# Value products of a head pair made together, in alternating column halves, with four probability slots

## What is computed

```
lb = einsum('bthd,bshd->bhts', qb, k_b)
lb = lb + swapaxes(fq, 1, 2)[..., None] - cum_f_keys[:, :, None, :]
lb = where(causal[None, None], lb, -inf)
pb = softmax(lb, axis=-1)
ob = einsum('bhts,bshd->bthd', pb, v_b)
```

## Time and profile before

| | |
|---|---|
| median of 3 runs | 2182.43 us (2182.37 to 2182.81) |
| profiled execution | 2186.65 us |
| its span, first to last instruction | 2185.0 us |
| PE busy | 2060.1 us, 94% of the span |
| DVE busy | 1236.7 us, 57% |
| ACT busy | 910.8 us, 42% |
| POOL busy | 289.2 us, 13% |
| DMA | mean 89 GB/s |

### The profile page before, as it was taken

The page is one execution under the profiler, slowest core; times in us unless marked ns, Lnnn a source line. Parts: engine busy times, 40 slices in busy tenths (PEclk is TensorE's granted clock), DMA queues, the critical chain, the costliest instruction groups (busy, mean ns, idle before and its releaser), DMA issues. The chain is left out here.

```text
span 2185.0 us, 26996 instructions
## 1 busy us (share of the span) xinstructions
PE 2060.1 (94%) x9546; PEld 1634.7 (75%) x9546; DVE 1236.7 (57%) x1910; ACT 910.8 (42%) x1403; POOL 289.2 (13%) x380
## 2 busy tenths in 40 slices
PE   8999998999999999999999988898887998999997
PEld 6666666888888677688888857787765677888886
DVE  3666556888677565756664353766556544333333
ACT  4333735444322443544442254565446624222222
POOL 0032501011000010000000012666410001000000
PEclk9999999999999999999999999999998999999999
DMA  5511023666454322233233212011110022233321
GB/s 171 147 47 39 1 68 102 193 194 193 134 173 136 106 87 78 67 96 96 96 107 106 86 38 78 30 30 39 59 39 1 1 87 77 96 96 96 116 94 51
DMA packets 52779, 193.93 MB, mean 89 GB/s; under 512 B 5808, under 2 KB 8528, under 8 KB 52312
## 3 DMA queue, kind: packets, MB, share of 16 engines
q1 hardware_dynamic: 44824, 165.18, 23.9%
q0 software_dynamic: 7344, 27.27, 4.0%
q10 hardware_dynamic: 528, 0.40, 0.1%
HBM read 189.15 MB, written 3.68 MB: 88 GB/s over the span
## 5 line engine op out<-in xcount | busy, mean ns | idle before, releaser
L196 PE MATMUL psum<-xH,w_hi 128*128 128x512 f32 x1800 | 729.1, 405 | 42.8 <-DVE xL L1377 22.1
L196 PE MATMUL psum<-xL,w_hi 128*128 128x512 f32 x1800 | 712.1, 396 | 0.0
L196 PE MATMUL psum<-xH,w_lo 128*128 128x512 f32 x1800 | 711.7, 395 | 0.0
L166 DVE TENSOR_TENSOR w_lo<-w_raw,w_hi 128x1024 fp32r<-128x1024 f32 (+1 forms) x273 | 357.0, 1308 | 365.4 <-ACT w_hi L160 365.0
L160 ACT ACTIVATE w_hi<-w_raw 128x1024 fp32r<-128x1024 f32 (+1 forms) x273 | 303.3, 1111 | 420.1 <-PE psum L196 410.8
L196 PEld LDWEIGHTS psum<-xH,w_hi 128*128 128x128 f32 x1800 | 344.4, 191 | 142.0 <-DVE xL L1377 37.7
L196 PEld LDWEIGHTS psum<-xH,w_lo 128*128 128x128 f32 x1800 | 344.4, 191 | 74.1
L196 PEld LDWEIGHTS psum<-xL,w_hi 128*128 128x128 f32 x1800 | 344.8, 192 | 71.4 <-issue 3.1
L196 PE MATMUL psum<-hidH,w_hi 128*128 128x512 f32 x528 | 206.2, 391 | 0.0
L196 PE MATMUL psum<-hidH,w_lo 128*128 128x512 f32 x528 | 205.4, 389 | 0.0
L196 PE MATMUL psum<-hidL,w_hi 128*128 128x512 f32 x528 | 205.4, 389 | 0.0
(11 more groups left out here) (321 smaller groups left out, 2488.4 us busy)
## 6 DMA issues: line engine op xcount, KB each, us to landing
w_raw<-in_up SPq DMA_DIRECT2D x132, 512.0 KB, 3.5
w_raw<-in_down SPq DMA_DIRECT2D x48, 704.0 KB, 4.1
mod_raw<-in_mod POOLq DMA_DIRECT2D x48, 512.0 KB, 3.9
w_raw<-in_sb_in SPq DMA_DIRECT2D x26, 512.0 KB, 3.5
w_raw<-in_ev_in SPq DMA_DIRECT2D x23, 512.0 KB, 4.0
w_raw<-in_od_in SPq DMA_DIRECT2D x20, 512.0 KB, 3.5
w_raw<-in_ev_out SPq DMA_DIRECT2D x8, 512.0 KB, 3.6
w_raw<-in_od_out SPq DMA_DIRECT2D x8, 512.0 KB, 3.5
```

Of the source, the lines that this page charges most:

```text
L166: nc.vector.tensor_tensor(w_lo[:, s % SPLIT, 0:w.cols], raw[:, s, 0:w.cols], w_hi[:, s % SPLIT, 0:w.cols].bitcast(F32), ALU.subtract).then ...
L196: mm = nc.tensor.matmul(acc, a[:, slot % SPLIT, cut], b[:, k0 + k, :], start=start and n == 0, stop=stop and n == 2)
```

## The change

The value products of the two heads of a pair are made in one call, at the step of the second head (steps 6, 8, ... 36), with the matmuls of the two heads taking turns over the key blocks. `pv_b` counts pairs instead of units. The transposed probabilities get four slots instead of two: the two of `pTb`, and two in columns 1024 to 1279 of the four rows of `w_raw`. ACT's copy of unit u waits from unit 4 on, for the pair of unit u - 4.

```diff
+        pT_b = (pTb[:, 0, :, :], pTb[:, 1, :, :], raw[:, :, KD * P:(KD + 1) * P], raw[:, :, (KD + 1) * P:(KD + 2) * P])
+        assert NB == RAW and (KD + 2) * P <= CHUNK
...
                 def prob_out(u):
                     kind, i, h = units[u]
                     if kind == "b":
-                        dst = pTb[:, u % 2, 0:i + 1, :]
-                        if u >= 2:
-                            act.wait_ge(a["pv_b"], u - 1)
+                        dst = pT_b[u % 4][:, 0:i + 1, :]
+                        if u >= 4:
+                            act.wait_ge(a["pv_b"], u // 2 - 1)
...
                         m = (s - 13) // 8
-                        act.wait_ge(a["pv_b"], 8 * (m + 1))
+                        act.wait_ge(a["pv_b"], 4 * (m + 1))
...
-                def values_b(u):
-                    _, i, h = units[u]
-                    m = u // 8
-                    pe.wait_ge(a["prob_out"], u + 1)
-                    if u % 8 == 0 and m >= 2:
+                def values_b(n):
+                    _, i, h0 = units[2 * n]
+                    m = n // 4
+                    pe.wait_ge(a["prob_out"], 2 * n + 2)
+                    if n % 4 == 0 and m >= 2:
                         pe.wait_ge(a["o_b_hi"], m - 1)
                     for j in range(i + 1):
-                        mm = nc.tensor.matmul(bank[6 + m % 2][rows(h), blk(i)], v_tm[:, j, h * HD:(h + 1) * HD],
-                                              pTb[:, u % 2, j, :], start=j == 0, stop=j == i)
+                        for e in range(2):
+                            mm = nc.tensor.matmul(bank[6 + m % 2][rows(h0 + e), blk(i)], v_tm[:, j, (h0 + e) * HD:(h0 + e + 1) * HD],
+                                                  pT_b[2 * (n % 2) + e][:, j, :], start=j == 0, stop=j == i)
                     mm.then_inc(a["pv_b"], 1)
...
-                    if PV <= s < UNITS + PV:
-                        values_b(s - PV)
+                    if PV <= s < UNITS + PV and (s - PV) % 2:
+                        values_b((s - PV) // 2)
```

## The result

The changed kernel takes 2171.18 us in the median (five runs, 2169.34 to 2172.14), against 2182.43 of the kernel before in five runs beside it (2180.35 to 2183.41): a ratio of 0.9948, with a 95% interval of 0.9933 to 0.9962. That is 11.3 us less, between 8.3 and 14.6. The forecast was 2170.8.

A forecast was written before the change was run, and what follows sets the result against it. PE alone was taken to bound the kernel from 116 to 218 us. Gains of 9.6 us there and 2.0 us behind sum to 11.6, taken off the median 2182.43: 2170.8 us, range 2167 to 2175.

The forecast's parts named there:

- The time of a pair's call: Value products, line 858: calls of 4, 8, 12, 16 records take 0.36, 0.58, 0.80, 1.03 us.
- The rival at 137 ns a record: Value products: weight loads run in series at 137 ns, so no change, 2182.5 us; chance 0.02.
- The sum of the projection: Pairs 0 to 11, steps 5 to 27: three rounds of 3.27 us saved, less 0.2, gives 9.6 us.
- The shape changes around a call: Array shape switches before and after each value product call: 0.13 us of the 0.49 for 2 records.
- The second head: Other column half in a pair's call: nearly free, 0.02 us a call, 0.2 us for twelve.
- Pair 12: Step 29: gains nothing; up to 0.36 us goes, but filler matmuls wait for ACT to empty bank 1 at 218.15.
- The tail: Pairs 13 to 15 (steps 31, 33, 35): 2.0 us, between 0 and 2.8, reckoned from ACT's waits, three ended by four slots.
- A second engine: Rival: DVE or ACT takes over as limit, half of the 9.6 us remains, 2177 to 2178 us; chance 0.06.
- The halves do overlap: Denied by a rival: accumulating products don't overlap, only the calls' fixed part is gained, 3.6 us, 2178.8 us; chance 0.03.
- a drain at each change of half: Rival, value products: array drains between halves, 0.20 us a record, four rounds lose 10 us, 2193 us; chance 0.03.
- The clock: Whole program: one or two stretches at 1.2 GHz more or fewer shift the time 1.7 to 3.4 us either way.
- the sum of 11.6: Whole change: 9.6 us from steps 5 to 27 plus 2.0 us from steps 31, 33 and 35.

The follow-up runs named there:

- the first profile: Profile of the changed kernel as first measured, against the kernel before: median 2171.18 us, ratio 0.9948.
- the repetition: The changed kernel measured once more with no edit: median 2170.76 us, ratio 0.9943 to the kernel before.
- the second mixer: Changed kernel with line 1684's loop alternating halves and the second mixer's key-value heads taken in turn: 2158.48 us, ratio 0.9884 to the kernel before.
- the kernel with heads in blocks: Changed kernel with loops swapped, all blocks of the even head, then all of the odd: 2171.49 us, ratio 0.9947 to the kernel before.

## Why the prediction was right

The bound, PE alone through the projection, was right: 109.92 us became 99.49, and a second engine shows in it at one place only. The time of a pair's call was right to 0.01 us for each size, because line 890 had shown the same form. The rule of the Trainium skill (TensorE: Matmul & The Clock Gate, Part 3, The mechanism), that a weight load overlaps matmuls in flight only where the row group differs, doesn't hold here: the loads of line 861 last 137 ns and use all rows, and 16 records take 1.02 us. Even in one half alone the records follow every 0.11 us, in less than a load's 137 ns. The rival at 137 ns a record would have had 2.2 us.

**The sum of the projection**, 9.6 us, was 10.4 in the first profile, with its slow first step, and 10.7 in the repetition. Two of its terms were small by a little, and a third was right for the wrong reason:
- The shape changes around a call are worth 0.20 us and not 0.13. I had taken 0.08 us from the last transpose to the projection, from a step with a single transpose; after several it is less. With four and no value product, it is 0.41 us from the first transpose to the projection (136.56 to 136.97) and 0.31 to its next matmul (137.28). With a value product it is 0.59 before it (139.85 to 140.44) and 0.33 behind (141.25 to 141.58): 0.20 more. After a single transpose the 0.08 holds without a value product, but with one it is 0.26 (146.65 to 146.91) and not 0.20, and 0.34 behind against 0.32: 0.20 again. For twelve calls that is 0.8 us.
- The second head costs 0.01 us a call and not 0.02: 0.1 us. With the 0.06 us of pair 12 (below) the sum is 10.6 us.
- **Pair 12** failed as put. I had taken the fillers to wait for ACT's copy that ends at 218.15. They don't: here they start at 208.32, while that copy runs from 207.85 to 208.45. They write bank 1, and the copy behind which I put them empties bank 0. The 0.36 us was there, but it was spent two instructions earlier, where PE's transposes found another copy of ACT not yet done:

```profile
206.26 1.12 PE L842 MATMUL psum<-ev_hT 64*128 64x512 f32 x2
207.61 0.41 PE L850 MATMUL psum<-ident,logits 128*128 128x128 f32 x2 [0.23 <-ACT pTb L601]
207.96 0.44 PE L861 MATMUL psum<-pTb,v_tm 128*64 128x128 f32 x4
208.32 0.94 PE L943 MATMUL psum<-ident,mean_of 128*128 128x128 f32 x6
```

From logits to transposes it is 1.35 us instead of the usual 1.05: 0.30 of 0.36 lost. The value of the term, nothing, was right for the wrong reason.

**The tail**, 2.0 us, was 2.4 in the repetition, where the clock stayed up, and 0.9 in the first profile, where 1.55 went to the clock. Its size was right and its reason half wrong. I had reckoned it by ACT's waits that the slots would end. The slots alone give 0.00 us, and pairs without them keep 1.8 of the 2.4. What counts there too is that PE issues less; ACT's waits were the consequence of PE's length, and only once PE is shorter are the slots worth their 0.6 us. In the repetition one of the three waits is still there, 0.32 us, now for the transposes:

```profile
217.53 0.60 ACT L601 ACTIVATE w_raw<-psum 128x512 f32<-128x512 f32 x1 [0.32 <-PE psum L850]
```

**The rivals.** A second engine did not take over: DVE kept 21.0 us of waiting for PE. The halves do overlap, in accumulation as well; a drain at each change of half, the way to a slower kernel, would have made a call of 16 records over 3 us long, and it is 1.02. **The clock** was the doubt of the range, and it behaved so: stretches at 1.2 GHz moved in and out between executions of the same kernel.

**Luck.** The two stretches of the repetition together gain 13.1 us, 1.5 more than the sum of 11.6, while the medians show 11.3 and 11.9. So that the forecast came within 0.4 us of the median is in part luck: terms a little too small met a median gain that is smaller than that of the stretches. Part of this second difference is again the clock. The kernel before ran at mean clocks from 0.977 to 0.984 in its 15 runs beside the repetition, and the repetition at 0.977 to 0.979; against the eight runs at these values (median 2183.1) its gain is 12.3 us. The 0.8 us left lie inside the interval, and why the clock differs stays open.

## What to carry to other kernels

Where products have only 64 output partitions (or 64 input partitions in separate banks), put those of the two halves of the array next to each other: the second costs 0.01 us a call here, and four records of the other half are within PE's reach even without strict alternation. Look for it first where PE issues without waiting, since there the gain comes off the end in full; where a chain of other engines is close (the second mixer), 12 of 17 us came through. Before giving memory to more buffers, ask who ends the wait that they remove: here it was the length of PE's own queue.

## What the runs showed of the hardware that I had not expected

- Row halves overlap too: the logits of two heads, 64 partitions each, in two banks, take 1.06 us together against 1.05 alone.
- PE runs up to about four records of one half beside the other's when they stand in blocks: calls of 8 records in two blocks take 0.60 us against 0.59 alternating, calls of 16 take 1.51 against 1.02.
- After a single transpose the next projection matmul starts 0.08 us later. After four it starts 0.41 us after the first; as their own starts take up 0.17 + 0.11 + 0.11 us of that, it is about 0.03 after the last.
- PE at half clock costs what PE had to issue: 1.55 us in the tail, but the repetition and the kernel with heads in blocks, at mean clocks of 0.977 and 0.982, are within 0.7 us in the median, although the second's two stretches were 3.2 us longer.
